# Gathering the expert rows of 32 dense tokens in place of 64, with the row work dealt to the last chunk and the next norm's rows in spent activation slots

## The reference, cut to what matters

```
def block(args):
    xi, ei, gi = args                        # tokens, expert numbers, gates
    act = gelu(einsum('td,ted->te', xi, u_tab[ei])) * gi
    return einsum('te,ted->td', act, v_tab[ei])
...
x = x + g2 * peer(h, w_q, keys, u_tab, v_tab)
h = rmsnorm(x, norm_g) * (1 + scale) + shift      # the next layer's norm
y = rmsnorm(x, final_g)                           # behind layer 1
```

## Time and profile before

| | before |
|---|---|
| time, median of 3 runs | 4288.07 us (4282.43 to 4294.07) |
| the profiled execution | 4287.76 us, span 4286.0 us |
| TensorE busy | 3901.2 us, 91% of the span |
| VectorE busy | 3037.2 us, 71% |
| GpSimd busy | 1907.1 us, 44% |
| ScalarE busy | 688.5 us, 16% |
| moved by DMA | 1169.31 MB, of it 679.58 MB by the gathers' queue and 445.02 MB by SyncE's queue |

### The profile page before, as it was taken

How to read it: one execution, slowest core, us unless ns; L and a number is a source line. 1 busy time by engine, 2 the same in 40 slices (tenths; PEclk the granted TensorE clock), 3 DMA queues, 4 the chain that set the end, 5 groups by cost and what they waited for, 6 DMA issues and landing times. The chain is left out here.

```text
span 4286.0 us, 46161 instructions
## 1 busy us (share of the span) xinstructions
PE 3901.2 (91%) x16342; PEld 2318.6 (54%) x16342; DVE 3037.2 (71%) x6236; ACT 688.5 (16%) x1432; POOL 1907.1 (44%) x1654
## 2 busy tenths in 40 slices
PE   8986889999999999899979997998989999999897
PEld 3643656686444444444347875577844444444442
DVE  6747535897877777778763146489788777777777
ACT  4122411162000000000023122104500000000000
POOL 0002300086776677776600000005767677777673
PEclk9997899999999999999989999999999999999999
DMA  4212741269999999999922105014899999999996
GB/s 176 90 51 99 272 178 37 67 178 351 401 418 420 420 420 420 418 415 420 415 95 69 59 20 128 20 55 123 275 399 406 420 420 420 419 418 416 413 418 258
DMA packets 375715, 1169.31 MB, mean 273 GB/s; under 512 B 35833, under 2 KB 120281, under 8 KB 364042
## 3 DMA queue, kind: packets, MB, share of 16 engines
q0 software_dynamic: 184960, 679.58, 39.1%
q1 hardware_dynamic: 107856, 445.02, 27.4%
q10 hardware_dynamic: 82684, 41.95, 3.4%
HBM read 1116.99 MB, written 48.37 MB: 272 GB/s over the span
## 5 line engine op out<-in xcount | busy, mean ns | idle before, releaser
L607 PE MATMUL banks<-h_dense_T,blocks 128*128 128x320 f32 x4096 | 1143.6, 433 | 3.2 <-ACT dense_act L452 3.2
L655 PE MATMUL banks<-blocks,picked_T 128*128 128x512 f32 x2048 | 991.0, 628 | 0.0
L607 PEld LDWEIGHTS banks<-h_dense_T,blocks 128*128 128x128 f32 x4096 | 778.4, 191 | 391.4 <-issue 104.6
L428 POOL DMA_INDIRECT expert_rows<-in_pk_u_dram,expert x640 | 823.0, 1286 | 355.4 <-DVE own_dots L912 175.5
L937 DVE SCALAR_TENSOR_TENSOR acc<-expert_rows,expert_weight,acc 128x1024 f32<-128x1024 f32 x628 | 794.3, 1284 | 257.1 <-DMA expert_rows<-in_pk_v_dram,expert 252.0
L912 DVE CUSTOM_DVE_ANT_0 expert_rows<-expert_rows,h_rows 128x1024 f32<-128x1024 f32 x640 | 774.4, 1225 | 268.2 <-DMA expert_rows<-in_pk_u_dram,expert 265.1
L428 POOL DMA_INDIRECT expert_rows<-in_pk_v_dram,expert x640 | 799.8, 1250 | 348.2 <-DVE acc L937 182.2
L655 PEld LDWEIGHTS banks<-blocks,picked_T 128*128 128x128 f32 x2048 | 385.3, 198 | 620.6 <-issue 620.6
L646 PE MATMUL banks<-blocks,picked_T 128*64 128x512 f32 x1024 | 297.0, 657 | 173.2 <-DVE picked_T L898 172.9
L452 ACT ACTIVATE dense_act<-banks 128x320 f32<-128x320 f32 x246 | 107.5, 438 | 2061.5 <-PE banks L607 2061.4
L416 POOL TENSOR_SCALAR expert_rows<-iota,picked_T 128x128 f32<-128x128 f32 x320 | 220.4, 707 | 412.5 <-ACT picked_T L458 377.4
(11 more groups left out here) (528 smaller groups left out, 3912.3 us busy)
## 6 DMA issues: line engine op xcount, KB each, us to landing
blocks<-in_pk_u_turned_dram SPq DMA_DIRECT2D x256, 512.0 KB, 6.5
blocks<-in_pk_v_dram SPq DMA_DIRECT2D x256, 512.0 KB, 6.5
ada_block<-in_ada_rest_dram SPq DMA_DIRECT2D x32, 1280.0 KB, 7.4
gates_dram<-shared ACTq DMA_DIRECT2D x40, 1024.0 KB, 6.0
shared<-gates_dram SPq DMA_DIRECT2D x32, 1280.0 KB, 10.5
blocks<-in_pk_w_q_dram SPq DMA_DIRECT2D x32, 512.0 KB, 3.6
expert_rows<-in_pk_u_dram,expert POOLq DMA_INDIRECT x640, 13.0
expert_rows<-in_pk_v_dram,expert POOLq DMA_INDIRECT x640, 13.5
```

The costliest lines, as they stand in the source:

```text
L428: pool.indirect_dma_start(out=rows[:, r % RING, :], out_offset=None, in_=table, in_offset=bass.IndirectOffsetOnAxis(ap=idx[:, at_:at_ + 1] ...
L607: mm = pe.matmul(dense_dots(c), u[:, k * P:(k + 1) * P], HT[:, k, 0:DENSE], start=(k == 0), stop=(k == KD - 1))
L655: mm = pe.matmul(ps[:, at_:at_ + HALF], wt[:, c % WEIGHED, z * P:(z + 1) * P], v[:, half_ * HALF:(half_ + 1) * HALF], start=(c == 0), stop ...
```

## The change

- `OWN` becomes 32. `DENSE` is 352, `WAYS` 4, the own unit 32 + 32 gathers, `ROWS` 576. The split tile has 96 tokens: a part of 64 in bank 4, as before, and a part of 32 in bank 5, whose sums are four quarters of the features (256 columns each) on four groups of 32 array columns.
- `ROWS_DONE` goes from 123 to 127: the rows are spread over all 128 chunks. `rows_by` deals (576 - 14)/231 for each unit of a pass in place of (640 - 14)/227.
- `GAPS` are spaced by 5 in place of 4.
- `gain`, `scale` and `shift` lie in activation slots that are free after chunk 123, and their load waits for 124 weighed chunks (and in layer 0 for all rows but 6). The squares' scrap output goes to the own tokens' input slot.
- `normalize` is cut in two (`mean`, `normalize`) and its parts are interleaved with `add_sums`. In layer 1 tile 0 is normalized inside the last chunk.

```diff
-ROWS_DONE = 123
+ROWS_DONE = 127
+NORMS_AT = 124
-OWN = 64
+OWN = 32
-GAPS = (4, 9, 13, 17, 21, 25, 29, 33)
+GAPS = (5, 10, 15, 20, 25, 30, 35, 40)
...
-        gain, scale, shift = rows[:, 5, :], rows[:, 6:8, :], rows[:, 8:10, :]
-        junk = rows[:, 0, :]
+        spent = [(c - EXTRA) % AHEAD for c in range(P - AHEAD, NORMS_AT)]
+        norms = dense_act[:, spent[0]:spent[-1] + 1, :].rearrange("p b n -> p (b n)")
+        gain = norms[:, 0:D]
+        scale, shift = (norms[:, n * D:(n + 2) * D].rearrange("p (g d) -> p g d", g=2)
+                        for n in (1, 3))
+        junk = H[:, NR, :]
...
-            sp.wait_ge(row_used, ROWS)
+            sp.wait_ge(weighed, NORMS_AT)
+            if layer == 0:
+                sp.wait_ge(row_used, ROWS - 6)
...
-                if j == 0:
-                    act.wait_ge(row_used, ROWS)
...
             for c in range(P):
                 weigh(c)
+                if layer == 1 and c == P - 1:
+                    mean(0)
+                    dve.wait_ge(next_in, 16)
+                    normalize(0)
...
-            for j in range(NR):
+            for j in range(layer, NR):
+                mean(j)
+            for j in range(layer, NR):
                 normalize(j)
             add_split()
-            for z in range(WHOLE):
-                add_sums(z)
-                normalize(NR + z)
-            normalize(NT - 1)
+            add_sums(0)
+            mean(NR)
+            add_sums(1)
+            normalize(NR)
+            for j in (NR + 1, NR + 2):
+                mean(j)
+            for j in (NR + 1, NR + 2):
+                normalize(j)
```

More of the change, by code:

```diff
@@ L317, in experts @@
         g_row = cand[:, :, :].rearrange("p (g h) n -> p g (h n)", g=2)
-        gain, scale, shift = rows[:, 5, :], rows[:, 6:8, :], rows[:, 8:10, :]
-        junk = rows[:, 0, :]
+        spent = [(c - EXTRA) % AHEAD for c in range(P - AHEAD, NORMS_AT)]
+        assert spent == list(range(spent[0], spent[0] + len(spent)))
+        norms = dense_act[:, spent[0]:spent[-1] + 1, :].rearrange("p b n -> p (b n)")
[3 more added lines that the diff above has]
+        junk = H[:, NR, :]
         HTN = shared[:, 0:KD * TOK].rearrange("p (k t) -> p k t", k=KD)
@@ L553, in next_turned @@
                                    ACT.Copy).then_inc(next_out, 1)
-            for j in range(NR):
-                square(j)
-                square_root(j)
+            square(0)
+            if layer == 0:
+                square(1)
+                square_root(0)
+            else:
+                square_root(0)
+                square(1)
+            square_root(1)
+            square(2)
             if layer == 0:
@@ L560, in _ @@
                     next_turned(j)
[L561 to L567, removed]
+            square_root(2)
+            square(3)
+            square(4)
+            square_root(3)
+            square_root(4)
             if layer == 0:
-                next_turned(NT - 1)
+                for j in range(NR, NT):
+                    next_turned(j)
         @block.tensor
@@ L981, in add_sums, with mean @@
                 add_to_x(t)
-            def normalize(j):
-                t = LAST[j]
-                g = group_of(t)
+            def mean(j):
                 dve.wait_ge(squared, j + 1)
@@ L990, in normalize @@
                 dve.reciprocal(ms[:, j:j + 1], ms[:, j:j + 1]).then_inc(ms_ready, 1)
+            def normalize(j):
+                t = LAST[j]
+                g = group_of(t)
                 dve.wait_ge(rooted, j + 1)
```

## The result

| | before | after |
|---|---|---|
| time, median | 4285.44 us (4 runs) | 4313.9 us (4310.84 to 4317.56, 4 runs) |
| ratio to before | | 1.0072, 95% interval 1.0057 to 1.0086 |
| span of the profiled execution | 4286.0 us | 4315.8 us |
| TensorE busy | 3901.2 us, 91% | 4097.1 us, 95% |
| VectorE busy | 3037.2 us, 71% | 2900.9 us, 67% |

What follows compares the result with a forecast made beforehand. Bytes bound the loops, with TensorE at 10% of slack. Loop -10, stands +8, ahead +21, copies +1, behind +4 make +24 us on 4287.76: 4312 us, its own range 4287 to 4350, the whole range 4258 to 4368.

Steps and rivals of the forecast that it cites:

- What is late next: In the chunk loops: with 64 gathers fewer in a layer, TensorE is what is late, no longer the rows.
- The dots: L607 in the loops, 352 columns for 320: 4.84 us for 4.40, +0.44 in each of 103 passes.
- The narrow group: At L646, four added matmuls of 256 columns with 32 columns of weights each: +0.50 us a pass.
- the upper bound: For the added matmuls at L646: what L646 has beyond two passes, 0.13, paid a second time: 0.59 us.
- The stands: TensorE standing in the loops: 4 us a layer, +8 in all, beside 2.8 for the slow first pass.
- Ahead of the loop: Before each loop: spreading gates of 32 more tokens and eight larger dots, +10.7 us a layer; own tokens' copies +0.5.
- Behind the loop: From the sums' end E: last norm at E + 20.5 in layer 0 (+2.0), E + 13.8 in layer 1 (+2.4).
- The DMA share: Sign in the profile after: a share in the loop near 0.92, with about 385 GB/s.
- (a): Rival: narrow groups fill L646's spare 0.13 us, addition 0.31, no stands in first passes: 4255 us; chance 0.13.
- (b): Rival: the loops' waits stay, caused by the gates' load itself, about 12 times a layer: 4390 to 4475 us; chance 0.08.
- (c): Rival: the narrow matmuls at L646 go only two at a time, 1.01 us, +131: 4443 us; chance 0.04.
- (d): Rival: TensorE is not the limit and the time follows the bytes: about 4160 us; chance 0.03.

## Why the prediction was right, and where not

4312 was forecast, 4313.9 measured. The 2 us flatter the sum: it was +24 on the profiled 4287.76, and the rise is 28.5 us by the medians and 29.8 by the spans. Point by point:

- **What is late next.** Right. TensorE took over from the rows, its wait for `weigh` went from 172.9 to 3.5 us, and leaving work out on one side and on the other (4176 and 4110 us) shows both limits directly.
- **The dots.** 4.84 us forecast, 4.83 measured, about 2 us less over both layers.
- **The narrow group.** The term was sized too low: 0.50 forecast, 0.57 measured, 18 us over both layers. I scaled L2255's rate rightly (bare, 0.43 for eight records, as the run with three narrow parts shows) but took only 0.07 for the second width, which costs 0.14, as much as the 0.13 that L646 already spent beyond its two passes; the upper bound, 0.59, was the better reading. The estimate from the Trainium skill (TensorE: Matmul & The Clock Gate, Measured speedup vs the span model), 0.57, agrees with the changed kernel in size alone. Its 3.07 is the page's figure for four tiles packed by rows, where these are packed by columns, and by it three narrow parts would take, as an estimate, 3 x 0.56 = 1.7 us. They take 1.43: the measurement decides, and the lost time belongs to the change of width and not to the packing.
- **The stands.** Sized too high, by some 10 us over both layers, which hid the last point. I kept 2.8 us for a slow first pass and allowed 4 us for others in each layer. The first pass ran at full clock, since its own wait had shrunk to 0.34 and 0.75 us, and there was one stand of 1.1 to 1.5 us and 0.6 at the fold, about 2 us a layer. The bound of 0 for stands, not the value taken, was near. Loop: 1153.0 forecast with the stands, 1156.2 and 1155.9 measured.
- **Ahead of the loop.** 11.2 forecast in each layer; 12.0 and, behind layer 0's end, 9.2 measured. That they agree is in part luck, for not all of it lies in the experts stage. In layer 0 the stage's first matmul (the queries) comes 3.5 us later, behind a mixer that the change does not touch (before, then after):

```profile
669.75 0.98 PE L587 MATMUL banks<-h_dense_T,blocks 128*128 128x384 f32 x1 [1.43 <-PEq L107]
```

```profile
673.23 0.98 PE L598 MATMUL banks<-h_dense_T,blocks 128*128 128x384 f32 x1 [1.43 <-PEq L107]
```

  Over all the traces this start lies anywhere from 661.2 to 675.3; the kernel before with 32 own tokens has it at 668.65 and begins to spread at 880.84, ahead of the 881.20 of the kernel before:

```profile
880.84 0.55 PE L633 MATMUL banks<-expert_rows 128*128 128x128 f32 x1 [1.17 <-DVE expert_rows L887]
```

  In layer 1 the stage's start is also 3.5 us later, counted from the end of layer 0's norm; it is 543.0 to 543.8 us behind it in the kernels with 64 own tokens and 544.5 to 546.4 in those with 32, and why stays open. The stages themselves grew by 8.6 and 5.8 us. The spreading grew by 10.4 and 8.1, forecast 10.7; the nine chunks of dots ahead of it and the own tokens' copies, for which I had put 0 and 0.5, lengthened the way to it by 0.7 and 0.6. From its end to the loop it is 2.6 and 2.7 us shorter, where I had put nothing.
- **Behind the loop.** `add_split` came at E + 1.0 and E - 2.0 (forecast + 1.3 and - 1.9), the last norm of layer 0 ended at E + 20.5 and the last of layer 1 at E + 13.7 (forecast 20.5 and 13.8). The small additions of the split tile grew by 1.8 (3.22 us for 1.41, forecast + 1.5), off by 0.3. In layer 1 the last output is 2.3 us later behind its loop than before, forecast 2.4.
- **The DMA share.** Wrong. I had expected 0.92 in the loop; it stayed at 0.95 to 1.03 in the stretches of 100 us with dots while the rate fell towards what the pass needs, 3.78 MB/9.94 us = 380 GB/s.
- **The rivals.** (a), the addition cheaper than bare passes, was excluded by the 0.57. (b), stands made by the gates' load, by the unbroken passes of the changed kernel, and for the kernel before by 4195 us without that load. (c), two at a time, by the pass of 9.94. (d), time by bytes, would need TensorE below 9.0 us a pass, where it takes 9.94; with TensorE's work left at 8.94 the same cut in gathers did give 4110 us.

So the narrow group was 18 us too cheap, and the stands and slow first passes that did not come gave 10 back, the dots 2. The experts stages ahead of the loops were put 8 us too high, and a later start of both stages, 7 us together, made that good. Errors that cancelled brought +24 within 6 us of the rise in the spans, and as the profiled execution of the changed kernel, 4317.56, lies 3.7 above its median, the forecast of 4312 meets the median to 2. That closeness is luck. The sign and the mechanism rest on more: 9.77 us of bytes against 8.94 of TensorE before, 9.0 against 9.94 after.

The dealing of rows to the last chunk is the useful part of the change, and only with 64 own tokens. I did not weigh it apart from the split, with which it is worth nothing; 4257 us was open to the kernel before.

## What to carry to other kernels

Where two resources are both within some per cent of full, work moved from one to the other is worth no more than the gap between them. Add up each one's bare time for one pass, before and after; the larger of each pair is close to the pass (9.77 and 8.94 us before, 9.0 and 9.94 after). Look for the edits in a bundle that serve the limit which the bundle removes; apart from it they may be the gain. Before a matrix is cut into parts of unlike widths, count the changes of width on TensorE as a cost of every pass. And when a forecast agrees to 2 us, look at where each stage starts: part of the agreement can lie in code that was not changed.

## What the runs showed of the hardware

- A DMA share of 1.00 does not say that the DMAs are the limit. The changed kernel shows 0.98 to 1.00 at 373 to 387 GB/s and 1.03 at 410, while TensorE never waits for them; the kernel with rows by chunk 120 shows 1.02 at 406. The rate beside the share, and the waits, tell the cases apart.
- f32 matmuls with 32 columns of weights in four column groups run four side by side at the bare rate, 0.215 us for four of 256 columns. Going from 128 columns of weights to 64 or to 32 and back costs 0.34 to 0.35 us in a pass beyond the bare records (0.14 to 0.15 of it between the first start of the other width and the next start of 128), and a change between 64 and 32 on the way a further 0.14, in either order.
- In the changed kernel TensorE hardly waits, and its granted clock is 1.00 (2.4 GHz) over both loops. Before, it is 0.97 and 0.96 over the loops; a stand of 4.4 us cost 2.8 us more in the work behind it, at a granted clock of 0.50 and then 0.60 (1.2 GHz for most of the time from 3583 to 3590 us).
